# Weight loads of the last product stage in halves, the output's tail regrouped: a hybrid attention block on one core

## The reference

```python
h = rms_norm(x, norm_in_w)
proj = jnp.einsum('bsd,dc->bsc', h, w_in)          # queries, keys, values, gates, latents
out_a = swa_sink_attention(qa, ka, va, sinks_a) * jax.nn.silu(a_g)     # 16 heads of 64
out_b = mla_attention(qb_nope, qb_rope, kb_nope, kb_rope, vb) * jax.nn.silu(b_g)   # 8 heads
mixed = jnp.concatenate([out_a, out_b], axis=-1)   # 512 x 2048
x = x + jnp.einsum('bsc,cd->bsd', mixed, w_out)
return rms_norm(x, final_norm_w)
```

## Time and profile before

| | |
|---|---|
| time, median of 3 runs | 665.0 us (664.98 to 665.48) |
| the profiled execution's own time, and its span | 665.19 us, 663.4 us |
| TensorE busy | 653.5 us (99%) |
| VectorE, ScalarE, GpSimd busy | 437.9 us (66%), 332.4 us (50%), 273.3 us (41%) |
| TensorE's granted clock, mean | 0.995 |
| DMA | 81.96 MB, 124 GB/s over the span |

### The profile page before, as it was taken

The page is one execution under the profiler, slowest core; times in us unless marked ns, Lnnn a source line. Parts: engine busy times, 40 slices in busy tenths (PEclk is TensorE's granted clock), DMA queues, the critical chain, the costliest instruction groups (busy, mean ns, idle before and its releaser), DMA issues.

```text
span 663.4 us, 8807 instructions
## 1 busy us (share of the span) xinstructions
PE 653.5 (99%) x3126; PEld 548.2 (83%) x3126; DVE 437.9 (66%) x706; ACT 332.4 (50%) x625; POOL 273.3 (41%) x133
## 2 busy tenths in 40 slices
PE   9999999999999999999999999999999999999994
PEld 8888888888888888888888888988888888887883
DVE  6868132889694554564554566787652749989996
ACT  6833231311334664664663657767864443554545
POOL 0044443354344424424424416766778566030012
PEclk9999999999999999999999999999999999999998
DMA  8732333133213223123122313122022841487526
GB/s 300 278 121 87 105 99 100 66 125 96 95 66 121 69 81 111 64 77 114 65 95 96 98 62 127 52 78 74 24 87 74 327 162 54 172 306 255 205 104 254
DMA packets 21944, 81.96 MB, mean 124 GB/s; under 512 B 2448, under 2 KB 2704, under 8 KB 19856
## 3 DMA queue, kind: packets, MB, share of 16 engines
q1 hardware_dynamic: 18000, 72.88, 31.8%
q10 hardware_dynamic: 3904, 8.54, 3.8%
HBM read 77.22 MB, written 4.19 MB: 123 GB/s over the span
## 4 chain that ended last, share of the span: by engine, by line
PE 98%; DVE 1%; ACT 0%; issue 0%; ACTq 0%; DVEq 0%
PE bank L1424 29%; PE bank L1427 29%; PE bank L1428 29%; PE bank L1689 1%; PE bank L1568 1%; PE bank L1578 1%; PE bank L1675 1%; PE bank L1676 1%; PE bank L1454 1%; PE bank L1591 1%; PE bank L1590 1%; PE bank L1447 1%; PE bank L1444 1%; PE bank L1492 0%; PE bank L1487 0%; PE bank L1480 0%
## 5 line engine op out<-in xcount | busy, mean ns | idle before, releaser
L343 POOL TENSOR_TENSOR w_lo<-w_raw,w_hi 128x1024 fp32r<-128x1024 f32 x84 | 206.0, 2459 | 269.4 <-ACT w_hi L449 269.3
L1424 PE MATMUL bank<-x_hi,w_hi 128*128 128x512 f32 x496 | 193.7, 391 | 0.0
L1427 PE MATMUL bank<-x_hi,w_lo 128*128 128x512 f32 x496 | 193.3, 390 | 0.0
L1428 PE MATMUL bank<-x_lo,w_hi 128*128 128x512 f32 x496 | 193.2, 390 | 0.0
L449 ACT ACTIVATE w_hi<-w_raw 128x1024 fp32r<-128x1024 f32 x93 | 98.1, 1055 | 130.8 <-PE bank L1424 112.4
L1428 PEld LDWEIGHTS bank<-x_lo,w_hi 128*128 128x128 f32 x496 | 93.1, 188 | 19.8
L1424 PEld LDWEIGHTS bank<-x_hi,w_hi 128*128 128x128 f32 x496 | 93.2, 188 | 18.7 <-DVE mixed L1101 0.2
L1427 PEld LDWEIGHTS bank<-x_hi,w_lo 128*128 128x128 f32 x496 | 93.2, 188 | 18.0
L1424 PE MATMUL bank<-w_hi,mx_hi 128*128 128x512 f32 x128 | 50.3, 393 | 0.0
L1428 PE MATMUL bank<-w_lo,mx_hi 128*128 128x512 f32 x128 | 49.9, 390 | 0.0
L1427 PE MATMUL bank<-w_hi,mx_lo 128*128 128x512 f32 x128 | 49.9, 390 | 0.0
(11 more groups left out here) (245 smaller groups left out, 1236.3 us busy)
## 6 DMA issues: line engine op xcount, KB each, us to landing
w_raw<-w_stream SPq DMA_DIRECT2D x93, 512.0 KB, 3.3
t_raw<-w_pairs SPq DMA_DIRECT2D x15, 1024.0 KB, 4.8
y<-x_nat ACTq DMA_DIRECT2D x4, 1024.0 KB, 6.3
out<-y SPq DMA_DIRECT2D x6, 512.0 KB, 3.2
xs<-x_t SPq DMA_DIRECT2D x4, 512.0 KB, 5.2
mixed<-x_t SPq DMA_DIRECT2D x4, 512.0 KB, 5.1
t_raw<-w_pairs ACTq DMA_DIRECT2D x1, 1024.0 KB, 7.7
fw<-final_w ACTq DMA_DIRECT2D x4, 256.0 KB, 4.8
```

The source lines that it names most:

```text
L343: pool.tensor_tensor(w_lo[:, s % HL, :], w_raw[:, s % RAW, :], w_hi[:, s % HL, :].bitcast(F32), ALU.subtract)\
L1424: ins = pe.matmul(dst, ah, bh, start=start, stop=False, skip_group_check=goes_on)
L1427: pe.matmul(dst, al, bh, start=False, stop=False, skip_group_check=goes_on)
L1428: return pe.matmul(dst, ah, bl, start=False, stop=stop, skip_group_check=goes_on)
```

## The change

Five things move; the work stays the same.

- SP loads visits 4 to 15 in two halves of 512 KB. The first half waits only for the first rise of `t_used` in visit `v - 4`, the second for the second, as the whole load did.
- ScalarE's two squares move from behind visit 10's high parts to behind visit 12's, the table load to behind visit 13's.
- TensorE makes M7 of visit 14 (pair 0) after M6 of visit 15 instead of before M1 of visit 15.
- In the tail GpSimd scales two blocks of tile 1 ahead of its last `gained`, ScalarE one block in place of two or three; VectorE's additions, row sums and scalings stand in another order, and VectorE and GpSimd trade blocks.
- SP stores tile 1 in three parts (512, 512 and 1024 columns), tile 0 in one transfer of 1024 KB and tile 3 in one. Tile 2 is stored as before.

The diff:

```diff
--- before.py
+++ after.py
@@ -290,6 +290,7 @@
         o_done, o_evac, o_squared, o_gained, o_rest, o_root = sem("o_done"), sem("o_evac"), sem("o_squared"), sem("o_gained"), sem("o_rest"), sem("o_root")
         o_recip, stored = sem("o_recip"), sem("stored")
         left, right = ([sem(f"{side}{t}") for t in range(TOK)] for side in ("left", "right"))
+        middle = {1: sem("middle1")}
 
         block = ctx.enter_context(nc.Block())
 
@@ -320,20 +321,28 @@
             sp.wait_ge(o_done, 8)
             sp.dma_start(t_raw[3][:, :, :], w_pairs[3, :, :, :]).then_inc(t_landed[3], 16)
             for v in range(4, VISITS):
-                if v == 11:
-                    sp.wait_ge(m_done, 6)
-                else:
-                    sp.wait_ge(t_used, 2 * v - 6 if v < 11 else 2 * v - 8)
-                sp.dma_start(t_raw[v % 4][:, :, :], w_pairs[v, :, :, :]).then_inc(t_landed[v % 4], 16)
-            for t in TILES_DONE[:3]:
+                for g in range(2):
+                    if v == 11:
+                        sp.wait_ge(m_done, 6 if g else 2)
+                    else:
+                        sp.wait_ge(t_used, (2 * v - 7 if v < 11 else 2 * v - 9) + g)
+                    two = slice(2 * g, 2 * g + 2)
+                    sp.dma_start(t_raw[v % 4][:, two, :], w_pairs[v, :, two, :]).then_inc(t_landed[v % 4], 16)
+            sp.wait_ge(left[1], 1)
+            sp.dma_start(out[0, P:2 * P, 0:SEQ], y[:, 1, 0:SEQ]).then_inc(stored, 16)
+            sp.wait_ge(middle[1], 1)
+            sp.dma_start(out[0, P:2 * P, SEQ:CE], y[:, 1, SEQ:CE]).then_inc(stored, 16)
+            sp.wait_ge(middle[1], 2)
+            sp.wait_ge(right[1], 1)
+            sp.dma_start(out[0, P:2 * P, CE:], y[:, 1, CE:]).then_inc(stored, 16)
+            for t in TILES_DONE[1:3]:
                 sp.wait_ge(left[t], 2)
-                sp.dma_start(out[0, P * t:P * t + P, 0:CE], y[:, t, 0:CE]).then_inc(stored, 16)
                 sp.wait_ge(right[t], 2)
-                sp.dma_start(out[0, P * t:P * t + P, CE:], y[:, t, CE:]).then_inc(stored, 16)
+                sp.dma_start(out[0, P * t:P * t + P, :], y[:, t, :]).then_inc(stored, 16)
             for c in (2, 3):
                 sp.wait_ge(right[2], c - 1)
                 sp.dma_start(out[0, 2 * P:3 * P, SEQ * c:SEQ * c + SEQ], y[:, 2, SEQ * c:SEQ * c + SEQ]).then_inc(stored, 16)
-            sp.wait_ge(stored, 16 * 10)
+            sp.wait_ge(stored, 16 * 9)
 
 
         @block.gpsimd
@@ -424,8 +433,6 @@
             for q in range(2):
                 pool.wait_ge(o_squared, 8 + q + 2)
                 gained(2 * q + 1, 2)
-            pool.wait_ge(o_squared, 13)
-            gained(0, 3)
 
             def scale(n, t, c, gains, side):
                 pool.wait_ge(o_recip, n + 1)
@@ -433,10 +440,13 @@
                 ys = y[:, t, SEQ * c:SEQ * c + SEQ]
                 pool.tensor_tensor(ys, ys, fin[:, t, 2:3].to_broadcast([P, SEQ]), ALU.mult).then_inc(side[t], 1)
 
+            scale(0, 1, 1, 8, middle)
+            scale(0, 1, 2, 9, middle)
+            pool.wait_ge(o_squared, 13)
+            gained(0, 3)
+            scale(1, 0, 3, 11, right)
             pool.wait_ge(y_added, 18)
-            scale(1, 0, 3, 11, right)
-            pool.wait_ge(y_added, 19)
-            scale(2, 3, 1, 8, left)
+            scale(2, 3, 2, 10, right)
 
 
         @block.scalar
@@ -723,7 +733,7 @@
             def part_high(v, g):
 
                 if g == 0 and v < 8:
-                    act.wait_ge(t_landed[v % 4], 16 * (v // 4) + 16)
+                    act.wait_ge(t_landed[v % 4], 32 * (v // 4) + 16)
                 else:
                     act.wait_ge(t_summed, v + 1 if v < 8 else 2 * v - 6 - (g == 1))
                 if v == 0:
@@ -793,10 +803,11 @@
                     act.wait_ge(p_low, 8)
                     for n in range(2, 4):
                         act.dma_start(fw[n][:, :], final_w[:, SEQ * n:SEQ * n + SEQ]).then_inc(fws_landed, 16)
-                if v == 10:
+                if v == 12:
                     for q in range(2):
                         act.wait_ge(y_added, 7 + q)
                         square(2 * q + 1, 2, 8 + q)
+                if v == 13:
                     act.activation(preloaded[:, :], eps[:, :], ACT.Sqrt)
 
             def root(t, rest, squared):
@@ -816,13 +827,11 @@
 
             last_square(1, 3, 10, 10)
             root(1, 1, 10)
-            scale(0, 1, 2)
-            act.wait_ge(o_gained, 9)
-            act.activation(y[:, 1, 2 * SEQ:3 * SEQ], y[:, 1, 2 * SEQ:3 * SEQ], ACT.Copy, scale=fin[:, 1, 2:3]).then_inc(right[1], 1)
+            scale(0, 1, 1)
             last_square(0, 3, 11, 12)
             last_square(0, 2, 12, 14)
             root(0, 3, 12)
-            scale(1, 0, 2)
+            scale(1, 0, 1)
             last_square(3, 3, 13, 17)
             root(3, 2, 13)
             scale(2, 3, 1)
@@ -1271,7 +1280,7 @@
             def part_sums(v):
 
                 raw = t_raw[v % 4]
-                dve.wait_ge(t_landed[v % 4], 16 * (v // 4) + 16)
+                dve.wait_ge(t_landed[v % 4], 32 * (v // 4) + 16)
                 if v < 8:
                     dve.tensor_tensor(raw[:, 2:4, :], raw[:, 0:2, :], raw[:, 2:4, :], ALU.subtract).then_inc(t_summed, 1)
                 else:
@@ -1386,7 +1395,7 @@
                 dve.wait_ge(o_recip, n + 1)
                 dve.wait_ge(o_gained, gains)
                 ys = y[:, t, SEQ * c:SEQ * c + SEQ]
-                dve.tensor_scalar(ys, ys, fin[:, t, 2:3], None, ALU.mult).then_inc(right[t], 1)
+                dve.tensor_scalar(ys, ys, fin[:, t, 2:3], None, ALU.mult).then_inc(left[t], 1)
 
             dve.wait_ge(fws_landed, 32)
             rest(1, 1, 10)
@@ -1396,22 +1405,23 @@
             add(0, 2, 4, 7)
             add(0, 3, 2, 9, 5)
             reciprocal(0, 1)
-            scale_gain(0, 1, 3)
             add(0, 2, 2, 9, 11, op=ALU.subtract)
             add(0, 2, 0, 10, 13, op=ALU.subtract)
+            scale_gain(0, 1, 3)
+            rest(3, 0, 13)
             add(2, 2, 5, 11)
+            reciprocal(1, 0)
+            scale(1, 0, 1, 8)
             add(3, 3, 5, 11, 4)
-            rest(3, 0, 13)
             add(3, 3, 7, 12, 16)
-            reciprocal(1, 0)
             scale_gain(1, 0, 2)
             add(2, 3, 3, 13, 6)
+            reciprocal(2, 3)
+            scale(2, 3, 1, 8)
             add(2, 2, 3, 13, 15, op=ALU.subtract)
-            reciprocal(2, 3)
             add(2, 2, 1, 14, 19, op=ALU.subtract)
+            rest(4, 2, 16)
             scale_gain(2, 3, 3)
-            rest(4, 2, 16)
-            scale(2, 3, 2, 10)
             reciprocal(3, 2)
             scale_gain(3, 2, 2)
             scale_gain(3, 2, 3)
@@ -1855,9 +1865,11 @@
                 pe.wait_ge(t_low[1], v + 1)
                 pe.wait_ge(p_low, v - 7)
                 last_of_pair(m6(v, 0), v)
-                if v == 15:
-                    last_of_pair(m5(v, 0), v)
-                last_of_pair(m7(v, 0), v)
+                if v == 13:
+                    m7(v, 0)
+            m7(14, 0)
+            last_of_pair(m5(15, 0), 15)
+            last_of_pair(m7(15, 0), 15)
             for product in (m1, m6, m5, m7):
                 for v in range(13, 16):
                     last_of_pair(product(v, 1), v)
```

## The result

The changed kernel takes 667.53 us (median of 7 runs, 666.78 to 668.4), the kernel before 665.09 beside it: ratio 1.0033, 95% interval 1.0024 to 1.0042. The profiled span grew from 663.4 to 665.4, 0.4 less than the time.

What follows compares the result with a forecast made beforehand. TensorE bounds the kernel until its last matmul, then queued stores set the end. TensorE's 0.45 us gain is spent in a DMA pause; traffic starting 1.4 later but 1.3 shorter gives +0.1: 665.1 us predicted, range 664.0 to 666.3.

Steps and rivals of the forecast that it cites:

- offset: Time from the end of TensorE's last matmul to the issue of tile 3's store, forecast at 1.68 us.
- The loads in two halves: Visit 8's second half lands at 601.3, VectorE's 0.52 us wait goes, and TensorE gains 0.45.
- VectorE is ready at 602.28: At visit 8 VectorE is ready only after the second half's landing at 601.3, with 0.9 us to spare.
- the gain of 0.45: TensorE's gain near 612: the 0.41 us gap and a little more, its end becoming 654.3.
- TensorE gains nothing: Rival: halves land as late as the whole load, time 665.7 us; chance 0.15.
- The tail work moved: At the end, tiles 1 and 0 are off the path; GpSimd's tile 3 block takes a 0.49 scaling from VectorE's tail.
- nothing stands behind it on GpSimd: GpSimd's third block of tile 3 starts at 653.1 and has until 655.95; two such blocks took 2.04 us.
- The single store of tile 3 is what counts: Tile 3's store is issued at 655.98, bytes flow from 656.8, and 2.10 MB take 5.1 us, to 661.9.
- I add no wait: VectorE's row sum of tile 2 at 654.9 finds ScalarE's square done near 654.6, so no delay is counted.
- ScalarE's squares and table load: Moved behind visits 12 and 13, 1.53 and 1.28 us fit into idle time of 2.21 per visit, costing nothing.
- The wait at visit 11: VectorE's 0.61 us wait for ScalarE's high part at 624.99 goes, helping its last low part end at 643.08.
- the conversions come late: Rival for slower: the moved ScalarE work delays VectorE's last conversions and TensorE waits, time 666.2 to 666.8 us; chance 0.10.

Runs made afterwards that it cites:

- x2: Changed kernel with each half load of visits 4 to 15 contiguous in device memory: 667.0 us, interval 1.0014 to 1.0032 against the kernel before.
- x3: Changed kernel with GpSimd's last block of tile 3 held back until VectorE has scaled blocks 0 and 1: 666.44 us.
- y4: Kernel before with the loads of visits 4 to 15 in halves, nothing else changed: 666.73 us, interval 1.0008 to 1.0026.
- z1: Changed kernel with GpSimd's last tile 3 block held back and VectorE's bank 3 subtraction put ahead of tile 3's reciprocal: 666.72 us.
- x4: Changed kernel with tile 3 stored in two halves again, tile 0 still in one: 666.17 us.
- z3: Kernel before with one edit, tile 3 leaving in one store that waits for all four blocks: 665.98 us.
- y1: Changed kernel with VectorE's multiplication of tile 1's block 3 back ahead of tile 0's two additions: 669.69 us.
- z4: Kernel before with only ScalarE's squares and table load moved and M7 of visit 14 behind M6 of visit 15: 665.32 us.
- z2: Changed kernel with whole loads, tile 3 in two stores, GpSimd's last block held back and bank 3's subtraction ahead of the reciprocal: 665.09 us.

## Why the prediction failed

The forecast span was 654.3 (TensorE's end) + 1.68 (offset) + 7.5 (from the store's issue to the end) = 663.5. In the profile it is 655.44 + 2.97 + 6.99 = 665.4. Two terms were wrong by more than a microsecond each, and the third by half of one the other way, which was luck: the end came about 1.0 us behind the last bytes (the DMA share is 0.38 in the second from 664), not 1.6. Beyond the span the prediction added 1.8 us and took off 0.2, where the profiled execution has 2.1 and the median lies on it; that is the rest of the 2.4 us between 665.1 and 667.5.

**The loads in two halves: the wait does not go.** The step that failed is "a load of 512 KB takes 3.3 us and lands at 601.3". That row belongs to other transfers: contiguous ones, at another place in the program. Visit 8's second half took 5.1 (598.29 to 603.39). Over the seven kernels with halves of the same layout it took 4.05 to 5.10 there, contiguous (x2) 4.57, and the whole load 4.65 to 4.89 in the six kernels that have it. "VectorE is ready at 602.28" failed too: it was ready at 602.96, 0.26 of that from ahead of the change and 0.4 by the longer wait at visit 4, which is 1.07 to 1.50 in the seven kernels, 0.90 to 1.18 with whole loads and 0.86 in x2. So even where the half was in time, the gain of 0.45 stayed out (x3: 0.14).

The rival *TensorE gains nothing* had this mechanism and put it at 0.45 of lost gain; but the halves also lose. Their gaps on TensorE run from 0.73 to 2.31 in the eight kernels that have them, and from 0.84 to 1.05 in the six that load whole, the kernel before among them. y4 puts the price of the halves alone at 0.0017 of the time, 1.1 us (0.5 to 1.7 by its interval), 0.2 of it outside the span. In z1 one late half is seen on its way from VectorE to TensorE. Why one kernel's halves land later than another's stays open.

The page DMA: Bandwidth & Descriptors of the Trainium skill (section Bandwidth), which the prediction weighed for the stores, speaks against the halves with its rule of 1 MiB and more; y4 agrees with it on the loads (halves cost 1.1 us). For the merged stores it brought nothing here: x4 (1.4 us faster with two) and z3 (0.8 slower with one) show that they cost the wait for the last block.

**The tail work moved: GpSimd's block was costed at nothing.** The step that failed is "nothing stands behind it on GpSimd", as if only GpSimd's time counted, with VectorE's scaling at 0.49. GpSimd ran beside that scaling, and it took 1.19. The price stood in the trace of the kernel before, in rows which the prediction did not look at, since they lie some sixty microseconds ahead of the tail. VectorE's difference of weight tiles took 2.31 where GpSimd was at work and 1.21 where it was not:

```profile
590.79 2.31 DVE L1276 TENSOR_TENSOR t_raw<-t_raw 128x1024 f32<-128x1024 f32 x1
...
598.74 1.21 DVE L1276 TENSOR_TENSOR t_raw<-t_raw 128x1024 f32<-128x1024 f32 x1
```

```profile
590.41 1.61 POOL L408 TENSOR_TENSOR y<-y,fw 128x512 f32<-128x512 f32 x1 [2.37 <-DVE t_lo L1287]
```

It ended (593.10) 1.08 behind GpSimd's instruction (592.02). In the Trainium skill, page SBUF — State Buffer, section "Who interferes with whom", an instruction of VectorE with two operands in SBUF and one of GpSimd that reads SBUF exclude each other for their whole length; it counts `tensor_scalar`, here the scaling by a column, among those that can run in a mode with two ports and contend, too, and excepts instructions with at most one operand in SBUF outside these modes, as the additions from PSUM are. The rows agree: in the meetings above VectorE ends 0.3 to 1.1 behind GpSimd's end. That the shared port is the cause is the page's word; the runs show the meeting and its price (x3). The page also says that the one issued first goes first; in y1 VectorE's row starts 0.04 ahead of GpSimd's and it came second all the same.

**The single store of tile 3 is what counts** was right as a mechanism, and so was its sum but for VectorE's part and the 0.5 above. In every kernel with one store and this SP order the end comes 7.0 us after its issue (tail minus offset in the table: 6.9 to 7.0), 0.5 less than forecast, and z3 lost 0.8 where the sum gives 1.0. With the forecast offset of 1.68 the tail would by this be 8.7, as before. So by estimate the store itself would be free there; it hands on in full what makes it late. Of the 1.29 by which it was late, 0.70 is the meeting at tile 3 (x3) and 0.33 the subtraction that stands behind tile 3's reciprocal and scaling (z1 against x3). Most of the remaining 0.26 is the row sum's wait for ScalarE's square: in z1 it starts 0.82 behind the last addition's start (657.06 and 656.24), where the forecast had 0.60. "I add no wait" was thus wrong too: the order on VectorE and ScalarE's square cost 0.6 together.

**What held.** ScalarE's squares and table load fit (idle 0.77 and 0.69 behind them in the profile after), and with M6 ahead of M7 they neither cost nor give any time that z4 can tell (its tail is 0.4 shorter in one profile). The wait at visit 11 went, as forecast, and the weight load at visit 15 still waits (0.28 for 0.20):

```profile
632.31 2.01 ACT L754 ACTIVATE t_hi<-t_raw 128x1024 fp32r<-128x1024 f32 x2 [0.77 <-DVE t_raw L1289]
634.34 1.28 ACT L811 ACT_TABLE_LOAD   x1
...
636.53 2.01 ACT L754 ACTIVATE t_hi<-t_raw 128x1024 fp32r<-128x1024 f32 x2 [0.69 <-DVE t_raw L1289]
```

The 0.61 gained there only made up for the 0.6 by which VectorE was late before: its last low part ends at 644.20, not near 643.1. Its chain also has a break that the prediction did not read, 0.53 for ScalarE's high part at 620.15; it stands in all fourteen profiles and changes no term of the sum. Tile 0's store, too, is off the path, though it is issued 1.6 later than forecast (653.69): its traffic ends at about 657.1, and tile 3's doesn't begin before 659. The rival for slower, *the conversions come late*, had the right sign and the wrong cause.

The pieces add up in the profiles: 0.26 from ahead of the change, 0.37 more gaps, 1.3 of tail, against 2.0 of span; 0.3 more of the time lies outside it. The mending of z2, which takes loads, meeting at tile 3, additions and store back, gives it all back within what its times can tell. What the meeting at tile 1 costs alone (1.35 for 0.75 in the profile after) was not isolated: z2 has it and loses nothing, and y1 moved it only into worse ones.

## What to carry to other kernels

Before work is given to an idle engine, look in the trace for the two engines side by side: an instruction's duration beside the helper's, not alone, is its price. A landing time belongs to a layout and a neighbourhood of transfers; split a load only if the piece that is waited for has been seen to land earlier. By this case's sums, merging the last stores is free as long as the last block is not late, and passes on every tenth of a microsecond by which it is.

## What was not expected of the hardware

- VectorE's instructions with all operands in SBUF wait for GpSimd's, also the scaling by a column: 1.18 to 1.37 for 0.49, 1.35 and 1.63 for 0.75, 2.31 for 1.21. GpSimd's wait for VectorE's as well: 1.49 for 1.04, 1.61 for 1.29. VectorE's additions from PSUM beside GpSimd take no longer (1.48 for two, 1.47 without it).
- A 512 KB load of 4 KB rows out of every 8 KB lands in 4.3 to 4.8 us by each kernel's median (3.5 at the fastest), a contiguous one in 3.2 (3.1), where issues are some 3 us apart. From visit 6's second half to visit 11, where issues are 1.4 and 2.7 apart, they take 3.7 to 6.3 and 3.7 to 4.7. A whole load of 1024 KB takes 4.6 to 5.0 there.
- An execution's time exceeds its span by 1.8 us in the kernels with whole loads and by 1.9 to 2.1 in those with halves; why is not shown.
